# Holding the expert weights or the rows in TensorE: gate and up turned round, in 70 blocks of one expert each

## What is computed

```python
def modulation(c, w_mod, b_mod):
    m = jax.nn.silu(c) @ w_mod + b_mod          # 6 x 1024 columns
    return jnp.split(m, 6, axis=-1)

# moe_ffn: 64 experts, each token goes to 8 of them (5120 token rows in all)
    def expert_block(args):
        tok, e = args
        xb = xpad[tok]
        hb = jax.nn.silu(xb @ w_gate[e]) * (xb @ w_up[e])   # 1024 -> 256
        return hb @ w_down[e]                                # 256 -> 1024
...
    shared = (jax.nn.silu(xf @ ws_gate) * (xf @ ws_up)) @ ws_down
    return (routed + shared).reshape(B, T, D)
```

## Time and profile before

| what | value |
|---|---|
| runs | 1082.56, 1085.35, 1085.72 us |
| median | 1085.35 us |
| profiled execution | 1084.15 us, its span 1082.3 us |
| granted TensorE clock, mean | 0.988 of 2.4 GHz |
| TensorE busy | 1022.1 us (94%) |
| VectorE, ACT, GpSimd busy | 330.1, 231.6, 164.2 us |
| moved by DMA | 321.64 MB, mean 297 GB/s |

### The profile page before, as it was taken

The page is one execution under the profiler, slowest core; times in us unless marked ns, Lnnn a source line. Parts: engine busy times, 40 slices in busy tenths (PEclk is TensorE's granted clock), DMA queues, the critical chain, the costliest instruction groups (busy, mean ns, idle before and its releaser), DMA issues.

```text
span 1082.3 us, 18470 instructions
## 1 busy us (share of the span) xinstructions
PE 1022.1 (94%) x7328; PEld 459.7 (42%) x7328; DVE 330.1 (30%) x825; ACT 231.6 (21%) x545; POOL 164.2 (15%) x238
## 2 busy tenths in 40 slices
PE   6999998999999999999999999999899999999574
PEld 2655556565455553334333333434333334333121
DVE  0112226764246763111121111121111112111177
ACT  1211106664123221111111111111111112111011
POOL 1000010300321111112122112122121121210000
PEclk9999999999999999999999999999999999999798
DMA  9964409300401657599999999999999999995596
GB/s 375 404 246 155 156 31 267 142 1 1 175 39 54 254 211 251 211 351 423 363 395 418 416 420 421 421 421 419 421 411 396 421 417 422 421 419 214 228 409 265
DMA packets 60222, 321.64 MB, mean 297 GB/s; under 512 B 10308, under 2 KB 10956, under 8 KB 32104
## 3 DMA queue, kind: packets, MB, share of 16 engines
q1 hardware_dynamic: 43184, 272.71, 62.9%
q0 software_dynamic: 14816, 43.34, 10.3%
q10 hardware_dynamic: 2136, 4.39, 1.1%
HBM read 299.86 MB, written 32.44 MB: 307 GB/s over the span
## 4 chain that ended last, share of the span: by engine, by line
PE 74%; DMA 13%; DVE 5%; SPq 5%; ACT 2%; issue 1%; POOL 0%; POOLq 0%; DVEq 0%; ACTq 0%
PE bank L1964 29%; PE bank L1984 14%; PE bank L1559 8%; DMA ring<-in_w_up 7%; PE bank L1731 5%; PE bank L1936 4%; DMA ring<-expert_rows 3%; PE bank L1823 3%; PE bank L1756 2%; PE bank L1742 1%; PE bank L1715 1%; PE bank L1829 1%; PE bank L1586 1%; DMA ring<-in_w_mod 1%; PE bank L1836 1%
## 5 line engine op out<-in xcount | busy, mean ns | idle before, releaser
L1964 PE MATMUL bank<-ring,reg_h 128*32 128x512 f32 x2592 | 333.1, 594 | 0.6 <-DMA ring<-in_w_up 0.4
L1964 PEld LDWEIGHTS bank<-ring,reg_h 128*32 128x32 f32 x2592 | 100.9, 110 | 181.1 <-issue 181.0
L1984 PE MATMUL bank<-ring,reg_y 128*32 128x512 f32 x1296 | 170.6, 594 | 1.5 <-ACT reg_y L989 1.5
L1964 PE MATMUL bank<-reg_p,reg_h 128*32 128x512 f32 x672 | 135.5, 598 | 3.8 <-DMA ring<-in_w_up 3.8
L1431 DVE TENSOR_TENSOR reg_h<-reg_p,bank 128x256 f32<-128x256 f32 x51 | 21.5, 421 | 338.4 <-ACT reg_p L1007 325.3
L704 POOL DMA_INDIRECT expert_rows<-reg_y,rowc x51 | 51.2, 1005 | 270.2 <-DVE reg_y L1415 258.4
L1007 ACT ACTIVATE reg_p<-bank 128x256 f32<-128x256 f32 x51 | 19.6, 384 | 322.5 <-PE bank L1964 322.5
L1559 PE MATMUL bank<-ring,reg_h 128*128 128x384 f32 (+2 forms) x256 | 84.3, 487 | 0.0
L1984 PEld LDWEIGHTS bank<-ring,reg_y 128*32 128x32 f32 x1296 | 47.5, 110 | 82.6 <-issue 78.6
L1415 DVE TENSOR_SCALAR reg_y<-bank,reg_p 128x512 f32<-128x512 f32 x51 | 38.3, 750 | 143.8 <-PE bank L1984 143.8
L1731 PE MATMUL bank<-ring,reg_h 128*128 128x512 f32 x160 | 70.3, 594 | 0.0
(11 more groups left out here) (269 smaller groups left out, 948.2 us busy)
## 6 DMA issues: line engine op xcount, KB each, us to landing
ring<-in_w_gate SPq DMA_DIRECT2D x51, 1024.0 KB
ring<-in_w_up SPq DMA_DIRECT2D x51, 1024.0 KB
ring<-in_w_down SPq DMA_DIRECT2D x51, 1024.0 KB, 17.6
ring<-in_w_mod SPq DMA_DIRECT2D x21, 1024.0 KB, 8.3
ring<-expert_rows SPq DMA_DIRECT2D x19, 1024.0 KB, 16.2
reg_p<-in_w_gate SPq DMA_DIRECT2D x13, 1024.0 KB
reg_p<-in_w_up SPq DMA_DIRECT2D x13, 1024.0 KB
reg_p<-in_w_down SPq DMA_DIRECT2D x13, 1024.0 KB
```

The costliest lines, as they stand in the source:

```text
L1964: last = pe.matmul(bank[2 + p][R * j:R * j + R, :], xg_t[:, p, k * P + R * j:k * P + R * j + R], w_gu(homes[n % SLOTS])[:, k], start=(k == ...
L1984: last = pe.matmul(bank[5 + hf][R * j:R * j + R, :], h_t[:, p, i * P + R * j:i * P + R * j + R], w_dn(homes[n % SLOTS])[:, i, 512 * hf:512 ...
```

## The change

The held and the streamed side of gate and up change places. A block now belongs to one expert: 58 experts have one block, the six ranks after the three fixed ones have two (`WIDE`), 70 in all. `block_gate_up` holds a 128 x 128 piece of the weights (every second of 256 columns of gate or of up) and streams the 128 rows of `xg_t`; its four outputs of 128 columns in one bank are gate and up with h's columns on partitions, so h comes out transposed. SiLU and product write `h_t` directly; the h transposes, their copies, `hh` and two semaphores go. Down uses the full-width helper `down` (L1832) of the shared expert. TensorE's order is gate-up(b), x transposes(b+2), down(b), one block after the other; ACT, VectorE, GpSimd and SyncE follow it. The x transposes always use banks 0 and 1.

Ahead of the loop: the bias of modulation groups 1 and 2 is put into `mod_rows` by GpSimd (zeros) and eight small DMAs on ACT's queue, and added by VectorE when it takes the group out of PSUM; `mod_bias` is left for group 0. `later_pieces(0)` moves from behind the first tile's projection into the second tile's. The Fourier maps write bank 5, the second scores no longer wait for ACT's last Fourier copy (the first transposes of probabilities into bank 5 do), and `fourier_y(2)` moves ahead of the last q and k transposes. `shared_down(2)` moves ahead of the first x transposes. The tables have 106 columns where they had 107.

```diff
-UNITS = (4,) * FIXED + (5,) * 6 + (4,) * 15 + (3,) * 22 + (2,) * 18
-ORDER = tuple(range(FIXED)) + tuple(FIXED + (i // 2 if i % 2 == 0 else E - FIXED - 1 - i // 2) for i in range(E - FIXED))
-FIRST = tuple(sum(UNITS[r] for r in ORDER[:n]) for n in range(E))
-TILES = tuple((n, u) for n, r in enumerate(ORDER) for u in range(UNITS[r]))
-NQ = len(TILES) // 4
-LAST = tuple((FIRST[n] + UNITS[r] - 1) // 4 for n, r in enumerate(ORDER))
-XGROUPS = 14
+DOUBLE = 6
+WIDE = tuple(range(FIXED, FIXED + DOUBLE))
+LARGE = tuple(range(FIXED + DOUBLE, FIXED + DOUBLE + (E - FIXED - DOUBLE) // 2))
+SMALL = tuple(range(E - 1, LARGE[-1], -1))
+
+
+def expert_order():
+
+    order = list(range(FIXED)) + [r for pair in zip(SMALL, LARGE + (None,)) for r in pair if r is not None]
+    step = (E - FIXED) // DOUBLE
+    for i, r in enumerate(WIDE):
+        order.insert(FIXED + 4 + step * i, r)
+    return tuple(order)
+
+
+ORDER = expert_order()
+BLOCKS = tuple(2 if r in WIDE else 1 for r in ORDER)
+FIRST = tuple(sum(BLOCKS[:n]) for n in range(E))
+EXPERT = tuple(n for n in range(E) for _ in range(BLOCKS[n]))
+NQ = len(EXPERT)
+LAST = tuple(FIRST[n] + BLOCKS[n] - 1 for n in range(E))
+XGROUPS = 9
...
-            for n in range(SLOTS, E + 1):
-                if n < E:
-                    e[n] = sp.value_load(eid[0:1, n:n + 1], min_val=0, max_val=E - 1)
-                    sp.wait_ge(s_g, LAST[n - SLOTS] + 1)
-                    load_gate_up(n, e[n])
-                if n > SLOTS:
-                    sp.wait_ge(s_y, LAST[n - 1 - SLOTS] + 1)
-                    load_down(n - 1, e[n - 1])
+            for n in range(SLOTS, E):
+                e[n] = sp.value_load(eid[0:1, n:n + 1], min_val=0, max_val=E - 1)
+                sp.wait_ge(s_g, LAST[n - SLOTS] + 1)
+                load_gate_up(n, e[n])
+                sp.wait_ge(s_y, LAST[n - SLOTS] + 1)
+                load_down(n, e[n])
...
             pool.memset(w_bd, 0.0).then_inc(s_clr, 1)
+            for q in range(1, 3):
+                pool.memset(mod_rows[q], 0.0).then_inc(s_clr, 1)
...
+            for b in range(NQ):
...
-                next_gather(b + 5)
-            next_scatter(NQ - 1)
+                next_scatter(b)
...
             act.activation(cw[:], cv[:], ACT.Exp, scale=-1.0).then_inc(s_cexp, 1)
+            act.wait_ge(s_clr, 5)
+            for q in range(1, 3):
+                for j in range(4):
+                    act.dma_start(mod_rows[q][R * j:R * j + 2, :],
+                                  b_mod[0:1, 2048 * q + 512 * j:2048 * q + 512 * j + 512].to_broadcast([2, 512])).then_inc(s_bias, 16)
...
             act.wait_ge(s_shx, T)
...
+            for b in range(NQ):
+                silu(b, b % 2)
+                if b + 2 < NQ:
+                    xt_half(b + 2, b % 2)
+                y_out(b)
...
                 dve.wait_ge(s_mpe, KD * (q + 1))
-                dve.tensor_copy(mod_rows[q], bank[(0, 0, 1)[q]][:, :]).then_inc(s_mrow, 1)
+                if q:
+                    dve.wait_ge(s_bias, 8 * 16)
+                    dve.tensor_tensor(mod_rows[q], mod_rows[q], bank[q - 1][:, :], ALU.add).then_inc(s_mrow, 1)
+                else:
+                    dve.tensor_copy(mod_rows[q], bank[0][:, :]).then_inc(s_mrow, 1)
...
-                at_least(dve, s_ht, b - 1)
-                dve.tensor_tensor(hh[:, p, :], sg[:, p, :], bank[2 + p][:, F:2 * F], ALU.mult).then_inc(s_h, 1)
+                at_least(dve, s_y, b - 1)
+                dve.tensor_tensor(h_t[:, p, :], sg[:, p, :], bank[2 + p][:, F:2 * F], ALU.mult).then_inc(s_h, 1)
...
-            def mod_bias(q):
+            def mod_bias():
                 for j in range(4):
-                    pe.matmul(bank[(0, 0, 1)[q]][R * j:R * j + R, :], ident[0:12, 4 * q + j:4 * q + j + 1].to_broadcast([12, R]),
-                              b_rows, start=True, stop=False)
+                    pe.matmul(bank[0][R * j:R * j + R, :], ident[0:12, j:j + 1].to_broadcast([12, R]), b_rows,
+                              start=True, stop=False)
                     last = pe.matmul(bank[(0, 0, 1)[q]][R * j:R * j + R, :], silu_w[:, k, :], buf[:, 512 * j:512 * j + 512],
-                                     start=False, stop=(k == KD - 1))
+                                     start=(q > 0 and k == 0), stop=(k == KD - 1))
                 last.then_inc(s_mpe, 1)
...
-                        mod_bias(q)
...
                     projection(t, (0, 1))
+                    if t == 1:
+                        later_pieces(0)
                     later_pieces(2 * t - 1)
                     qk_t(t - 1)
-                if t < T - 1:
+                if 0 < t < T - 1:
                     later_pieces(2 * t)
...
-                    if p:
-                        pe.wait_ge(s_fo, 4)
...
+                    elif b:
+                        pe.wait_ge(s_fo, 4)
...
-            def block_transposes(b, p, gathered, banks=(0, 1)):
+            def block_transposes(b, p, gathered):
+                at_least(pe, s_xa, b)
+                at_least(pe, s_xb, b)
-                    last = pe.transpose(bank[banks[k // 4]][:, (k % 4) * P:(k % 4 + 1) * P], v[:, k, :], ident)
+                    last = pe.transpose(bank[k // 4][:, (k % 4) * P:(k % 4 + 1) * P], v[:, k, :], ident)
...
-            def block_gate_up(b):
-
-                p = b % 2
-                tiles = [n for n, u in TILES[4 * b:4 * b + 4]]
-                pe.wait_ge(s_xa, b + 1)
-                pe.wait_ge(s_xb, b + 1)
-                at_least(pe, s_h, b - 1)
-                for n in sorted(set(tiles)):
-                    if FIRST[n] >= 4 * b:
-                        pe.wait_ge(*gate_up_in(n))
-                for k in range(KD):
-                    for j, n in enumerate(tiles):
-                        last = pe.matmul(bank[2 + p][R * j:R * j + R, :], xg_t[:, p, k * P + R * j:k * P + R * j + R],
-                                         w_gu(homes[n % SLOTS])[:, k], start=(k == 0), stop=(k == KD - 1))
+            def block_gate_up(b, p, home):
+
+                w = w_gu(home)
+                for i in range(2):
+                    for j in range(2):
+                        out = bank[2 + p][:, (2 * i + j) * P:(2 * i + j + 1) * P]
+                        for k in range(KD):
+                            last = pe.matmul(out, w[:, k, i, j:F:2], xg_t[:, p, k * P:(k + 1) * P],
+                                             start=(k == 0), stop=(k == KD - 1))
-            def block_down(b):
-                p = b % 2
-                tiles = [n for n, u in TILES[4 * b:4 * b + 4]]
-                pe.wait_ge(s_he, b + 1)
+            def block_down(b, p, home):
+                pe.wait_ge(s_h, b + 1)
-                if b % 2 == 0:
-
-                    pe.wait_ge(s_xa, min(b + 3, NQ))
-                    pe.wait_ge(s_xb, min(b + 3, NQ))
-                for n in sorted(set(tiles)):
-                    if FIRST[n] >= 4 * b:
-                        pe.wait_ge(*down_in(n))
-                for hf in range(2):
-                    for i in range(2):
-                        for j, n in enumerate(tiles):
-                            last = pe.matmul(bank[5 + hf][R * j:R * j + R, :], h_t[:, p, i * P + R * j:i * P + R * j + R],
-                                             w_dn(homes[n % SLOTS])[:, i, 512 * hf:512 * hf + 512], start=(i == 0), stop=(i == 1))
-                last.then_inc(s_y, 1)
+                down(home, (5, 6), h_t[:, p, :]).then_inc(s_y, 1)
...
             pe.wait_ge(s_shm, 1)
+            shared_down(2)
             block_transposes(0, 0, 16)
-            shared_down(2)
             shared_h_t(4)
...
             pe.wait_ge(s_shm, T - 1)
-            for b in range(0, NQ, 2):
-                if b:
-                    block_down(b - 2)
-                block_gate_up(b)
-                if b:
-                    block_down(b - 1)
-                if b + 1 < NQ:
-                    block_gate_up(b + 1)
-                block_h(b, 0)
+            for b in range(NQ):
+                n = EXPERT[b]
+                pe.wait_ge(s_xa, b + 1)
+                pe.wait_ge(s_xb, b + 1)
+                at_least(pe, s_h, b - 1)
+                if b == FIRST[n]:
+                    pe.wait_ge(*gate_up_in(n))
+                block_gate_up(b, b % 2, homes[n % SLOTS])
                 if b == 0:
                     pe.wait_ge(s_shm, T)
-                for n in range(b + 2, min(b + 4, NQ)):
-                    x_in(n)
-                if b + 1 < NQ:
-                    block_h(b + 1, 1)
-            block_down(NQ - 1)
+                if b + 2 < NQ:
+                    block_transposes(b + 2, b % 2, 16 * (b // 2 + 2))
+                if b == FIRST[n]:
+                    pe.wait_ge(*down_in(n))
+                block_down(b, b % 2, homes[n % SLOTS])
```

(48 more changed lines are left out.)

71 lines of the change are left out of this document (18 added, 53 removed).

## The result

The changed kernel takes 1334.99 us (median of 4 runs, 1333.36 to 1337.67) against 1085.53 us before: a ratio of 1.231, 95% interval 1.228 to 1.234. It is slower by 23%, as forecast. The forecast was 1297 us, its range 1273 to 1355, which holds the time; the likeliest case's own range ended at 1338.

What follows compares the result with a forecast made beforehand. TensorE was taken as the bound, transfers just behind. 1084.15 us, plus 215 for 70 blocks of 11.63 (814 against 598.9), minus 3 ahead of the loop, gave 1296, and 1297 as median; range 1273 to 1355.

Steps and rivals of the forecast that it cites:

- the likeliest case: Whole kernel: 70 expert blocks of 11.63 us make it slower, 1297 us, own range 1273 to 1338; chance 0.82.

Runs made afterwards that it cites:

- the moved quarter of gate-up: The changed kernel with contiguous held weights and the first quarter of the next block's gate-up put ahead of down: 1283.96 us, ratio 1.183.

## What to carry over

When held and streamed sides change places, count the held columns as well as the streamed ones: at 128 of each the load sets the time, and the 64 rows left out of the stream gave nothing back, while rows held can be packed in groups of 32. Cost a strided operand from a row of the same kind of instruction, and if there is none, keep its price in the range; a transpose is not such a row. A wait that is taken away is worth what is late next, and the name of that stands in the same timeline, a few rows on.

## What the runs showed of the hardware

- An fp32 matmul with 128 x 128 held and 128 streamed, record by record: 0.1116 us contiguous, 0.1177 with a step of two on the held side, 0.236 with a step of eight there, 0.233 (14.93 / 64) with a step of eight on the streamed side. Streaming 64 instead of 128, at step two: 0.1169.
- Transposes of 128 x 128 with a step of eight keep 0.110 us.
- A down of eight records took 3.51 us from its start to that of the next matmul when it started behind the wait for VectorE, 3.44 when it started behind the moved quarter of gate-up. The wait need not be the cause: in the changed kernel's chain the shared down at 388.69 also takes 3.51, behind two records that stream 36 columns, with no wait shown.
